# Two feed-forward input blocks computed tile by tile with tokens stationary

## The reference, cut to what matters

```python
h = h + rmsnorm(merged @ w_out, norm_mix_post)
n2 = rmsnorm(h, norm_ffn_pre)
gu = n2 @ w_ffn_in                                   # 1024 -> 2 * 2816
ff = (silu(gu[..., :2816]) * gu[..., 2816:]) @ w_ffn_out
h = h + rmsnorm(ff, norm_ffn_post)
```

## Time and profile before

| | us |
|---|---|
| median of 3 runs | 1178.14 |
| lowest, highest | 1177.74, 1179.59 |
| profiled execution, its time | 1177.23 |
| profiled execution, its span | 1175.4 |
| PE, DVE, ACT, POOL busy | 1060.0, 811.2, 389.8, 272.4 |

### The profile page before, as it was taken

One profiled execution on the slowest core, in us unless ns is written; L12 is line 12 of the kernel. 1 busy time (PEld: TensorE's weight loads), 2 busy tenths in 40 slices (PEclk: granted clock), 3 DMA queues, 4 the chain that ended last, 5 costly groups with the idle time before them and its releaser, 6 DMA issues.

```text
span 1175.4 us, 12637 instructions
## 1 busy us (share of the span) xinstructions
PE 1060.0 (90%) x4468; PEld 689.4 (59%) x4468; DVE 811.2 (69%) x1704; ACT 389.8 (33%) x724; POOL 272.4 (23%) x261
## 2 busy tenths in 40 slices
PE   8999699999998778798877777899999999999998
PEld 7888354544454233244322222359888878999986
DVE  5787868777877768787887776764555586555543
ACT  7674212202220111310211012045765445444532
POOL 0001345434444334433433433400000000000000
PEclk9999899999999999999999999999999999999999
DMA  9847999999999999999999999977434444555540
GB/s 346 337 168 270 393 375 398 422 421 421 422 420 422 421 421 421 421 421 421 418 420 422 410 421 416 421 271 267 144 143 144 162 161 161 180 180 181 183 174 36
DMA packets 55534, 371.91 MB, mean 316 GB/s; under 512 B 6192, under 2 KB 7344, under 8 KB 12080
## 3 DMA queue, kind: packets, MB, share of 16 engines
q0 software_dynamic: 36864, 268.45, 55.4%
q1 hardware_dynamic: 18608, 102.65, 23.7%
HBM read 370.03 MB, written 1.05 MB: 316 GB/s over the span
## 4 chain that ended last, share of the span: by engine, by line
PE 58%; DMA 29%; DVE 8%; issue 3%; ACT 1%; POOL 1%; DVEq 0%; POOLq 0%; ACTq 0%
DMA uv<-in_peer_uv,eidx 29%; PE bank L2123 13%; PE bank L1821 12%; PE bank L1823 12%; PE bank L1822 12%; PE bank L1893 4%; DVE uv L1509 3%; PE bank L1792 1%; DVE diag L1523 1%; POOL uv L696 1%; PE bank L2011 1%; DVE xn L1691 0%; DVE tmp L1684 0%; PE bank L1965 0%; PE bank L1932 0%
## 5 line engine op out<-in xcount | busy, mean ns | idle before, releaser
L2123 PE MATMUL bank<-uv,diag 128*128 128x512 f32 x1024 | 491.2, 608 | 100.4 <-DVE diag L1523 93.9
L1509 DVE SCALAR_TENSOR_TENSOR uv<-uv,xn 128x1024 f32<-128x1024 f32 x256 | 313.5, 1225 | 132.4 <-DMA uv<-in_peer_uv,eidx 129.9
L2123 PEld LDWEIGHTS bank<-uv,diag 128*128 128x128 f32 x1024 | 180.4, 191 | 375.9 <-issue 373.5
L696 POOL DMA_INDIRECT uv<-in_peer_uv,eidx x256 | 272.1, 1063 | 485.6 <-PE bank L2123 357.6
L1228 DVE TENSOR_TENSOR w_lo<-wraw,w_hi 128x2048 fp32r<-128x2048 f32 x71 | 162.3, 2290 | 119.5 <-ACT w_hi L772 119.4
L984 ACT ACTIVATE chosen<-chosen 128x1 f32<-128x1 f32 x256 | 51.8, 203 | 505.0 <-DVE uv L1509 504.7
L772 ACT CAST w_hi<-wraw 128x2048 fp32r<-128x2048 f32 x71 | 135.3, 1908 | 65.6 <-PE bank L1823 65.4
L1821 PE MATMUL bank<-nT_hi,w_hi 128*128 128x256 f32 x432 | 122.5, 284 | 0.8 <-DVE nT_lo L1249 0.8
L1822 PE MATMUL bank<-nT_lo,w_hi 128*128 128x256 f32 x432 | 122.3, 283 | 0.0
L1823 PE MATMUL bank<-nT_hi,w_lo 128*128 128x256 f32 x432 | 122.3, 283 | 0.0
L1523 DVE TENSOR_SCALAR diag<-const,chosen 128x128 f32<-128x128 f32 x256 | 89.1, 348 | 10.9 <-ACT chosen L984 10.7
(11 more groups left out here) (271 smaller groups left out, 1190.6 us busy)
## 6 DMA issues: line engine op xcount, KB each, us to landing
wraw<-in_ff_in SPq DMA_DIRECT2D x22, 1024.0 KB, 4.8
wraw<-in_ff_out SPq DMA_DIRECT2D x11, 1024.0 KB, 4.7
wraw<-in_query SPq DMA_DIRECT2D x4, 1024.0 KB, 5.2
uv<-in_peer_uv,eidx POOLq DMA_INDIRECT x256, 13.2
wraw<-in_in_q SPq DMA_DIRECT2D x2, 1024.0 KB, 9.0
wraw<-in_in_k SPq DMA_DIRECT2D x2, 1024.0 KB, 9.6
wraw<-in_pool_o SPq DMA_DIRECT2D x2, 1024.0 KB, 4.8
wraw<-in_sb_o SPq DMA_DIRECT2D x2, 1024.0 KB, 4.7
```

Source lines behind the costliest of these rows:

```text
L696: pool.indirect_dma_start(out=uv[:, RING_AT[n % RING], :], out_offset=None, in_=io["peer_uv"], in_offset=bass.IndirectOffsetOnAxis(ap=eidx ...
L1509: nc.vector.scalar_tensor_tensor(out=u, in0=u, scalar=1.0, in1=xn[:, head // PEER_HEADS, :], op0=ALU.mult, op1=ALU.mult, accum_out=hdot[he ...
L2123: mm = nc.tensor.matmul(acc[m][:, :], diag[:, n % RING, :], uv[:, RING_AT[n % RING], D + m * HALF:D + (m + 1) * HALF], start=(n % (ROWS // ...
```

## The change

Blocks `ff_in0` and `ff_in1` are computed with tokens stationary, one tile at a time (`ff_tokens`). Tile 0's part stands where `keep_warm` stood, ahead of the transposes of tile 1; tile 1's part stands behind them. The 256 weight columns of a block (128 gate, 128 up) move, and both blocks of a tile share one bank (`ff_t`). Silu and the gated product are taken with tokens on the partitions; two transposes a tile (`turn_h`) then bring the product into `hT`, ahead of blocks `ff_in2` and `ff_in3`. ACT and DVE round and subtract from that bank. The two blocks get split places of their own, and their casts and splits move forward; the slots of `ff_in2` to `ff_in4` become free with `out2_1b`. The rest of the feed-forward is as it was.

```diff
@@ -66,6 +66,7 @@
 PIECED = ("in1a", "in1b", "in2_vb")
 SLOT_AT = {name: (n + (2 if name in ("out1a", "out1b") else n > SPLIT_AT["out1b"])) % S_SLOTS for name, n in SPLIT_AT.items()}
 SLOT_OF = {name: SPLIT[n - S_SLOTS] for name, n in SPLIT_AT.items() if n >= S_SLOTS}
+SLOT_OF |= {f"ff_in{j}": "out2_1b" for j in (2, 3, 4)}
 SLOT_OF |= {"out1a": "in0a", "out1b": "in0b"}
 RING_AT = (1, 4, 2, 5, 0, 3, 6, 7)
 SPLIT_END, _parts = {}, 0
@@ -83,6 +84,8 @@
         return ("xq",) if name == "in2_x" else ("y_x", NT - 1, 1)
     if name.startswith(("in2_q", "in2_k")):
         return (name[4:5] + "2", int(part))
+    if name in ("ff_in0", "ff_in1"):
+        return ("ff_t", NT - 1)
     if name.startswith("ff_in"):
         return ("ff", int(name[5:]))
     if name.startswith("ff_out"):
@@ -243,8 +246,12 @@
     for t in range(NT):
         for n in range(2):
             use("w_out2", n, t)
-    both("n2T")
-    for j in range(FC):
+    for t in range(NT):
+        for h in range(2):
+            use("n2T", t, h)
+        use("ff_t", t)
+    for j in range(2, FC):
+        use("hT", j - 2) if j < 4 else None
         use("ff", j)
     for t in range(NT):
         for n in range(2):
@@ -335,6 +342,8 @@
         w_hi_first = place("w_hi_first", 122 * KB, [P, WB], F32R)
         w_lo_first = place("w_lo_first", 130 * KB, [P, WB], F32R)
 
+        w_hi_ff1 = place("w_hi_ff1", 54 * KB, [P, WB], F32R)
+        w_lo_ff1 = place("w_lo_ff1", 62 * KB, [P, WB], F32R)
         w_hi_out2 = place("w_hi_out2", 80 * KB, [P, WB], F32R)
         w_lo_out2 = place("w_lo_out2", 72 * KB, [P, WB], F32R)
 
@@ -517,6 +526,9 @@
         def four(ap):
             return ap.rearrange("p (c k) -> p c k", c=4)
 
+        def by_half(ap):
+            return ap[:, :].rearrange("p (j a k) -> p j a k", j=2, a=2)
+
         def two(ap):
             return ap.rearrange("p (c k) -> p c k", c=2)
 
@@ -549,6 +561,10 @@
 
             if name == "out2_1b":
                 return w_hi_out2[:, :], w_lo_out2[:, :]
+            if name == "ff_in0":
+                return w_hi_first[:, :], w_lo_first[:, :]
+            if name == "ff_in1":
+                return w_hi_ff1[:, :], w_lo_ff1[:, :]
             if name == "in2_va":
                 return w_hi_first[:, :], w_lo_first[:, :]
             s = SLOT_AT[name]
@@ -761,7 +777,7 @@
                     s = split[0]
                     assert SPLIT[s] not in PIECED
                     raw = wait_loaded(act, SPLIT[s])
-                    if s >= S_SLOTS and SPLIT[s] not in ("out0b", "in2_va", "out2_1b"):
+                    if s >= S_SLOTS and SPLIT[s] not in ("out0b", "in2_va", "out2_1b", "ff_in0", "ff_in1"):
 
                         done = last_product(SLOT_OF[SPLIT[s]])
                         if done:
@@ -1141,8 +1157,10 @@
                 for m in range(2):
                     src = wait_full(act, "w_out2", m, t)
                     half_square(src[:, :], 4, t, m)
+                    if (t, m) == (0, 0):
+                        act.wait_ge(merged_ready, 2 * NT)
+                        split_to("ff_in1")
                     if (t, m) == (1, 0):
-                        split_to("ff_in0")
                         for h in range(2):
                             round_tile("n2T", nT_hi, 0, h)
                 for m in range(2):
@@ -1153,12 +1171,17 @@
                 round_tile("n2T", nT_hi, 1, h)
             split_to("ff_in2")
             for j in range(FC + 1):
-                if j < FC:
+                if j < 2:
+                    src = wait_full(act, "ff_t", j)
+                    nc.scalar.activation(two(silu[:, j, :]), by_half(src)[:, :, 0, :], ACT.Silu).then_inc(silu_ready, 1)
+                elif j < FC:
                     src = wait_full(act, "ff", j)
-                    if j >= 2:
-                        wait_read(act, "ff", j - 2)
+                    wait_read(act, *(("ff_t" if j < 4 else "ff"), j - 2))
                     nc.scalar.activation(silu[:, j % 2, :], src[:, 0:S], ACT.Silu).then_inc(silu_ready, 1)
-                if j >= 1:
+                if j in (1, 2):
+                    src = wait_full(act, "hT", j - 1)
+                    nc.scalar.copy(hT_hi[:, 0:2, tok(j - 1)], two(src[:, 0:S])).then_inc(product_rounded, 1)
+                elif j > 2:
 
                     wait_read(act, "ff", j - 1)
                     nc.scalar.copy(hT_hi[:, j - 1, :], h32[:, (j - 1) % 2, :]).then_inc(product_rounded, 1)
@@ -1736,8 +1759,10 @@
             for t in range(NT):
                 for m in range(2):
                     gain_half(4, t, m, lambda m: ("w_out2", m, t))
+                    if (t, m) == (0, 0):
+                        split_to("ff_in0")
                     if (t, m) == (1, 0):
-                        split_to("ff_in0")
+                        split_to("ff_in1")
                         for h in range(2):
                             rest_tile("n2T", nT_lo, nT_hi, 0, h)
                 add_normed(4, t)
@@ -1753,15 +1778,27 @@
                 rest_tile("n2T", nT_lo, nT_hi, 1, h)
             split_to("ff_in2")
             for j in range(FC + 1):
-                if j < FC:
-
+                if j < 2:
                     dve.wait_ge(silu_ready, j + 1)
-                    if j >= 2:
-                        dve.wait_ge(ffT_ready, j - 1)
+                    src = bank[at("ff_t", j)[0]]
+                    nc.vector.tensor_tensor(two(h32[:, j, :]), two(silu[:, j, :]), by_half(src)[:, :, 1, :],
+                                            ALU.mult).then_inc(read_of("ff_t", j), 1)
+                elif j < FC:
+
+                    dve.wait_ge(silu_ready, j + 1)
+                    if j < 4:
+                        wait_full(dve, "hT", j - 2)
+                    else:
+                        dve.wait_ge(ffT_ready, j - 3)
                     src = bank[at("ff", j)[0]]
                     nc.vector.tensor_tensor(h32[:, j % 2, :], silu[:, j % 2, :], src[:, S:2 * S],
                                             ALU.mult).then_inc(read_of("ff", j), 1)
-                if j >= 1:
+                if j in (1, 2):
+                    dve.wait_ge(product_rounded, j)
+                    t = j - 1
+                    nc.vector.tensor_tensor(hT_lo[:, 0:2, tok(t)], two(bank[at("hT", t)[0]][:, 0:S]),
+                                            hT_hi[:, 0:2, tok(t)].bitcast(F32), ALU.subtract).then_inc(read_of("hT", t), 1)
+                elif j > 2:
                     dve.wait_ge(product_rounded, j)
                     nc.vector.tensor_tensor(hT_lo[:, j - 1, :], h32[:, (j - 1) % 2, :], hT_hi[:, j - 1, :].bitcast(F32),
                                             ALU.subtract).then_inc(ffT_ready, 1)
@@ -2282,12 +2319,35 @@
                             turn_merged(1)
                         if (t, n, p) == (1, 1, "a"):
                             turn_n2(0)
-            keep_warm(22, "n2T", 1, 0)
+            def ff_tokens(t):
+
+                for j in range(2):
+                    w = split_block(f"ff_in{j}")
+                    dst = bank[at("ff_t", t)[0]] if j else open_bank("ff_t", t)
+                    for c in range(KC):
+                        if j == 0 and c % (KC // 2) == 0:
+                            wait_read(pe, "n2T", t, c // (KC // 2))
+                        mm = product(dst[:, j * S:(j + 1) * S], parts(nT, ALL, c, tok(t)),
+                                     parts(w, ALL, slice(c * S, (c + 1) * S)), start=(c == 0), stop=(c == KC - 1))
+                mm.then_inc(full_of("ff_t", t), 1)
+
+            def turn_h(t):
+
+                wait_read(pe, "ff_t", t)
+                transposes(h32[:, t, :], "hT", t)
+
+            ff_tokens(0)
             turn_n2(1)
-            for j in range(FC):
-                channels_out(f"ff_in{j}", nT, "ff", j, turned="n2T" if j == 0 else None)
+            ff_tokens(1)
+            for j in range(2, FC):
+                if j < 4:
+                    turn_h(j - 2)
+                channels_out(f"ff_in{j}", nT, "ff", j)
+            for t in range(NT):
+                wait_read(pe, "hT", t)
             for j in range(FC // 2):
-                pe.wait_ge(ffT_ready, 2 * j + 2)
+                if j:
+                    pe.wait_ge(ffT_ready, 2 * j)
                 rows_out(f"ff_out{j}", (hT_hi, hT_lo), j == 0, j == FC // 2 - 1, 2 * j, lambda t, n: ("ff_out", t, n))
 
 
```

## The result

The changed kernel takes 1172.15 us (median of 4 runs, 1170.68 to 1173.33) against 1178.16 for the kernel before (also four runs, so not quite the 1178.14 of the table of before): ratio 0.9948, 95% interval 0.9935 to 0.9961. It is faster by 6.0 us where 5.1 were forecast, inside the range; the interval allows a gain of 4.6 to 7.7 us. The profiled execution took 1172.71 us, span 1170.9.

A forecast was written before the change was run, and what follows sets the result against it. The feed-forward was taken as PE-bound, with 8.02 us ahead of it where PE mostly waits for tile 1's norm. -5.76 + 0.58 + 0.05 = -5.1 us gave 1172.1 us (1173.0 against the median), range 1171.4 to 1175.6.

The forecast's parts named there:

- Part 1: Under tile 1's norm, tile 0's 48 matmuls at 0.120 us take 5.76 us and fit before tile 1's transposes.
- slip: Tile 0's products might end late before tile 1's transposes: 0.05 us booked, bounds 0 and 0.2.
- Rival A: Tokens-stationary matmuls are dear whatever their width: the change loses from 0.175 us each, 1183.4 us at 0.23; chance 0.04.
- Operands and hand-offs: Casts, splits and rest ready before `ff_tokens(0)` with 0.8 us slack; gated product ready before `turn_h(0)` with 1.4 us slack.
- B: `ff_tokens(0)` starts d late through late `ff_in1` or DVE queueing, losing d less 0.8 us; 1176 to 1179 us, chance 0.05.
- C: DVE gates tile 0 behind one more split, 0.9 us idle PE before `turn_h(0)`; 1174 us, chance 0.06.
- Part 2: Tile 1's products start at 983.09 and end at 988.85, where two blocks took until 994.61: gain 5.76 us.
- Part 3: Two new `turn_h` pairs of transposes on PE cost 0.29 us a pair, 0.58 in all; bounds nothing and 1.27.
- Edits at nothing: Removing `keep_warm`, earlier releases on SP's queue and the changed `ffT_ready` wait cost or gain nothing.
- Rival D: The clock falls to 1.2 GHz for tile 1's products, 11.5 us instead of 5.76: 1178.8 us, chance 0.02.

The follow-up runs named there:

- the late split: Changed kernel with the casts and splits of `ff_in0` and `ff_in1` both where that of `ff_in0` stood before: 1174.71 us, ratio 0.9974.
- the exposed form: Changed kernel with tile 0's part moved behind tile 1's transposes and the `keep_warm` turns back in its place: ratio 0.9994.
- the half cover: Changed kernel with only `ff_in0`'s half of tile 0 under the norm, then 12 `keep_warm` turns, `ff_in1`'s half behind tile 1's transposes: 1175.23 us, ratio 0.9965.

## Why the prediction was right

- **Part 1** held in place and price: 48 matmuls of 256 columns, tokens stationary, 0.120 us apart, transposes at the same 5.87 us. No slip where 0.05 was booked. Rival A had nothing behind it; the row for the form settles it. The Trainium skill (TensorE: Matmul & The Clock Gate, Back-to-back issue gap) has the gap between isolated matmuls grow with the moving columns alone; 109 ns for 256 is an estimate by its warm formula. The trace agrees on what sets it and has 11 ns more. For a stream in which each matmul has its weight load, as here, the same section says that this formula gives too much at 512 columns, which the trace doesn't bear out: 0.23 us against 0.216 by the formula.
- **Operands and hand-offs** held: slack 1.1 us before `ff_tokens(0)` (0.8 forecast), and no idle PE before `turn_h`. Rivals B and C did not occur; the late split shows what B costs, and that B's account was off: a start d late is not made good by the 0.8 us that the operands have in hand, but only by the 5.87 - 5.76 = 0.11 us between the cover and its products. A start 1.94 us late cost 1.83.
- **Part 2** held: tile 1's products at 8.02 us, as before.
- **Part 3** was sized too high: two transposes hold PE 0.14 us and the restart costs 0.08 more than a normal spacing of 0.12, so 0.22 us a pair and 0.44 in all, not 0.58. The record of one is 0.27 us here too, which says nothing of its cost in a stream.
- The sum for the profiled execution by these terms is -5.76 + 0.44 = -5.32, where the stretch shows 5.35.
- **The step that did not hold** is in "Edits at nothing": "The `keep_warm` turns filled waiting". They also held the clock, by 3.0 us in the profile without them, and in the kernel before they held it in only two profiles of four. The prediction read 1.00 in one profile and took it for every run. Rival D asked about the clock of the changed kernel, which stayed at 1.00 in three profiles; it was the old stream that lost it. Half of the executions at 1.5 us would make the missing 0.75 us of the gain, but four profiles don't fix that share. So the range held by its mechanism, which the stretches show, while the last 0.75 us lie within the noise of the run times.

## What to carry to other kernels

When PE waits for a norm of a second tile, give it the first tile's share of the next product: a gain equal to the matmuls moved, less the transposes that the new form adds, as long as their operands are early and they end before the next thing PE owes the chain. Moving the casts and splits forward was a third of it, and letting the products that need only the rounded part go first closed another 0.7 us. Count between two fixed points of PE in several profiles of both kernels before a difference of half a microsecond is explained.

## What the runs showed of the hardware

- Dummy matmuls did not always keep the clock up. In the kernel before, behind 44 records of identity matmuls in 5.1 us, 0.8 us idle, eight transposes and 0.8 us idle, it fell to 0.50 with the first products in two of four profiles. In the exposed form, the same without the second hole, and in the half cover, where the turns follow 24 products, it stayed at 1.00 in the one profile of each. Behind products, with the same transposes and a hole after them, it stayed at 1.00 in all four profiles (the changed kernel three, the late split one). That products hold it better than dummy turns is not shown by so few, and the streams differ in two things: the changed kernel has products in place of dummy turns, and no 0.8 us of idle PE before the transposes. No run separates them. The Trainium skill (TensorE: Matmul & The Clock Gate, Part 4: PE-mode transpose) says that transposes don't count as PE-busy; the two profiles that lost the clock behind transposes and idle time agree with it but can't tell the one from the other, and in the changed kernel the clock stayed at 1.00 through the same eight transposes.
- With PE idle for 2.84 us between products and transposes the clock went to 0.50 in the one profile taken, while PE was still idle; it stayed low for some 7 us and cost 2.5.
